# A delta-rule mixer whose level of 32 rows streams 128 columns per matmul instead of 64, with its banks of PSUM dealt out anew

## What is computed

```python
lmat = jnp.where(pos[:, None] > pos[None, :],
                 jnp.einsum('nbhid,nbhjd->nbhij', kb, kc) * decay, 0.0)
rhs = jnp.concatenate([vc * bc[..., None], kb * jnp.exp(gc)[..., None]], axis=-1)
sol = lax.linalg.triangular_solve(lmat, rhs, left_side=True, lower=True, unit_diagonal=True)
def step(s, inp):
    v_new = u_i - jnp.einsum('bhcd,bhde->bhce', w_i, s)
    s_next = s * gl_i[..., None, None] + jnp.einsum('bhcd,bhce->bhde', kd_i, v_new)
```

## Time and profile before

| | |
|---|---|
| median of three runs | 2609.36 us (2608.47 to 2612.84) |
| the profiled execution | 2613.24 us |
| its span, first to last instruction | 2611.4 us |
| TensorE matmul, busy | 2305.8 us (88%) |
| TensorE weight load, busy | 1528.2 us (59%) |
| VectorE, ScalarE, GpSimd, busy | 641.4, 475.2, 178.1 us |
| mean granted TensorE clock | 0.919 |
| `stage_delta`, first flip to the end of the chain | 1156.87 to about 1356 us |

### The profile page before, as it was taken

One profiled execution on the slowest core, in us unless ns is written; L12 is line 12 of the kernel. 1 busy time (PEld: TensorE's weight loads), 2 busy tenths in 40 slices (PEclk: granted clock), 3 DMA queues, 4 the chain that ended last, 5 costly groups with the idle time before them and its releaser, 6 DMA issues. The chain is left out here.

```text
span 2611.4 us, 26661 instructions
## 1 busy us (share of the span) xinstructions
PE 2305.8 (88%) x11220; PEld 1528.2 (59%) x11220; DVE 641.4 (25%) x1467; ACT 475.2 (18%) x879; POOL 178.1 (7%) x236
## 2 busy tenths in 40 slices
PE   6999696877999599889987899999979579999996
PEld 5855385565888475568876444454448444544453
DVE  2555112012220313652222211111110321111112
ACT  1222401112210224533331100000011110000000
POOL 1033001001110113300000000000000000000000
PEclk9999797998999799987787899999989879999998
DMA  6479542322442111010012899999944269999993
GB/s 191 159 257 334 198 170 72 125 69 66 160 163 69 65 65 65 33 65 1 1 44 118 342 427 427 428 427 427 427 185 161 97 259 427 427 427 428 427 427 157
DMA packets 120020, 575.55 MB, mean 220 GB/s; under 512 B 5153, under 2 KB 28282, under 8 KB 95322
## 3 DMA queue, kind: packets, MB, share of 16 engines
q1 hardware_dynamic: 118431, 570.59, 54.9%
q0 software_dynamic: 768, 2.02, 0.4%
q10 hardware_dynamic: 698, 1.18, 0.2%
HBM read 572.72 MB, written 1.05 MB: 220 GB/s over the span
## 5 line engine op out<-in xcount | busy, mean ns | idle before, releaser
L419 PE MATMUL linear_ps<-hT,ring 128*128 128x256 f32 x1344 | 300.2, 387 | 39.0 <-PEq L338 18.3
L419 PEld LDWEIGHTS linear_ps<-hT,ring 128*128 128x128 f32 x1344 | 260.6, 194 | 78.3 <-issue 41.7
L2423 PE MATMUL ex_u<-ring_extra,ex_xt 128*64 128x512 f32 x1024 | 224.9, 593 | 7.2 <-DMA ring_extra<-in_w 7.2
L2423 PE MATMUL ex_u<-ring,ex_xt 128*64 128x512 f32 x1024 | 225.0, 593 | 5.3 <-DMA ring<-in_w 3.9
L1657 PE MATMUL dl_front<-dn_src,ring 128*128 128x256 f32 (+1 forms) x512 | 177.5, 503 | 2.0 <-DVE dp_cv L1824 2.0
L2423 PEld LDWEIGHTS ex_u<-ring_extra,ex_xt 128*64 128x64 f32 x1024 | 76.3, 137 | 152.4 <-issue 152.2
L2423 PEld LDWEIGHTS ex_u<-ring,ex_xt 128*64 128x64 f32 x1024 | 78.0, 137 | 147.9 <-issue 147.9
L1106 PE MATMUL ffn_ps<-hT,ring 128*128 128x256 f32 x704 | 155.2, 384 | 5.9 <-PEq L338 5.9
L1106 PEld LDWEIGHTS ffn_ps<-hT,ring 128*128 128x128 f32 x704 | 135.8, 193 | 25.3 <-issue 6.3
L2512 DVE TENSOR_TENSOR ex_hid<-ex_sil,ex_u 128x512 f32<-128x512 f32 x32 | 34.6, 1081 | 435.9 <-PE ex_u L2423 435.9
L1657 PEld LDWEIGHTS dl_front<-dn_src,ring 128*128 128x128 f32 x512 | 99.3, 199 | 65.8 <-issue 58.9
(11 more groups left out here) (478 smaller groups left out, 2756.1 us busy)
## 6 DMA issues: line engine op xcount, KB each, us to landing
ring<-in_w SPq DMA_DIRECT2D x96, 2048.0 KB, 23.8
ring_extra<-in_w SPq DMA_DIRECT2D x96, 2048.0 KB, 25.1
ring<-in_ada_w SPq DMA_DIRECT2D x24, 2048.0 KB, 8.4
ring<-in_ffn_w_up SPq DMA_DIRECT2D x22, 1024.0 KB, 6.4
ring<-in_w_in SPq DMA_DIRECT2D x8, 2048.0 KB, 9.0
ring<-in_w_in_a SPq DMA_DIRECT2D x8, 2048.0 KB, 8.4
ring<-in_w_in_b SPq DMA_DIRECT2D x6, 2048.0 KB, 20.1
ring<-in_ffn_w_down SPq DMA_DIRECT2D x5, 2048.0 KB, 7.9
```

What stands on the lines that cost most here:

```text
L419: mm = pe.matmul(ps[:, q % banks, 0:n], w[:, k, j * P:(j + 1) * P], src[:, k, 0:n], start=k == 0, stop=k == kc - 1)
L2423: mm = pe.matmul(u[H * a:H * a + H, i, :], xt[:, b, k, H * a:H * a + H], w[a][:, 512 * k:512 * k + 512], start=k == 0, stop=k == KC - 1, s ...
```

## The change

Cross 0 and join 0 stream all 128 columns of `XN` and `XT` where they streamed two blocks of 32; the engines that read the products take the columns they want out of the wider tile, so they read as many elements as before. The results are placed in the full width of banks 5 and 3 (cross 0) and 4 and 5 (join 0). The near products of join 0 no longer fit beside them and move to the second half of bank 0, beside the output of the chain. Hence a new wait: from head 2 on, join 0 of head h waits until the output of head h-2 has been copied out. Cross 1 and join 1 keep their matmuls, in other banks. `part` goes. (The core of the diff; the reading sides of ScalarE and VectorE change in the same way.)

```diff
-        cross_ps = lambda k, d: ps[:, ((5, 3), (3, 4))[k][d], 0:T].rearrange("p (t n) -> p t n", t=4)
-        join_bank = lambda k, d: ((4, 5), (5, 3))[k][d]
-        join_ps = lambda k, d: ps[:, join_bank(k, d), 0:T].rearrange("p (t n) -> p t n", t=4)
-        near_ps = lambda d: ps[:, join_bank(0, d), T:T + P].rearrange("p (t n) -> p t n", t=4)
+        wide_cross_ps = lambda d: tiles_of(5 if d == 0 else 3)
+        cross_ps = lambda d: ps[:, 3 + d, 0:T].rearrange("p (t n) -> p t n", t=4)
+        wide_join_ps = lambda d: tiles_of(4 + d)
+        join_ps = lambda d: ps[:, 5 if d == 0 else 3, 0:T].rearrange("p (t n) -> p t n", t=4)
+        near_ps = lambda d: ps[:, 0, T + d * P:T + (d + 1) * P].rearrange("p (t n) -> p t n", t=4)
...
-                                mm = pe.matmul(cross_ps(k, d)[:, t, :], LT[g][:, m, :], part(d, XN[:, d, t, :]), start=True, stop=True)
+                                mm = pe.matmul(wide_cross_ps(d)[:, t, :], LT[g][:, m, :], XN[:, d, t, :], start=True, stop=True)
...
+                        elif h >= 2:
+                            pe.wait_ge(dl["o_taken"].sem, dl["o_taken"].at(h - 1))
...
-                                mm = pe.matmul(join_ps(k, d)[:, t, :], T1[:, k, d, t, :], part(1 - d, XT[g][:, m, :]), start=True, stop=True)
+                                mm = pe.matmul(wide_join_ps(d)[:, t, :], T1[:, k, d, t, :], XT[g][:, m, :], start=True, stop=True)
...
-                                ins = act.activation(T1[rows, k, d, :, cols], cross_ps(k, d)[rows, :, quad(i)], ACT.Copy)
+                                ins = act.activation(T1[rows, k, d, :, cols], wide_cross_ps(d)[rows, :, cols], ACT.Copy)
```

More of the change, by code:

```diff
@@ L1939, in stage_delta @@
         side_of = lambda i: slice(64 * i, 64 * i + 64)
-        def part(d, ap):
-            return ap.rearrange("p (a b n) -> p a b n", a=2, b=2)[:, :, d, :]
         @block.sync
@@ L1977, in _ @@
                             if k == 0:
-                                mm = pe.matmul(cross_ps(k, d)[:, t, :], LT[g][:, m, :], part(d, XN[:, d, t, :]), start=True, stop=True)
+                                mm = pe.matmul(wide_cross_ps(d)[:, t, :], LT[g][:, m, :], XN[:, d, t, :], start=True, stop=True)
                             else:
-                                mm = pe.matmul(cross_ps(k, d)[far, t, :], LT[g][near, m, far], XN[near, d, t, near], start=True, stop=True)
+                                mm = pe.matmul(cross_ps(d)[far, t, :], LT[g][near, m, far], XN[near, d, t, near], start=True, stop=True)
                         mm.then_inc(dl["z"].sem, dl["z"].tick())
@@ L1991, in _ @@
                                 pe.matmul(near_ps(d)[near, t, :], XT[g][near, m, near], T1[near, k, d, t, quad(3 * d)], start=True, stop=True)
-                                mm = pe.matmul(join_ps(k, d)[:, t, :], T1[:, k, d, t, :], part(1 - d, XT[g][:, m, :]), start=True, stop=True)
+                                mm = pe.matmul(wide_join_ps(d)[:, t, :], T1[:, k, d, t, :], XT[g][:, m, :], start=True, stop=True)
                             else:
-                                mm = pe.matmul(join_ps(k, d)[near, t, :], T1[far, k, d, t, near], XT[g][far, m, far], start=True, stop=True)
+                                mm = pe.matmul(join_ps(d)[near, t, :], T1[far, k, d, t, near], XT[g][far, m, far], start=True, stop=True)
                         mm.then_inc(dl["uv"].sem, dl["uv"].tick())
@@ L2056, in _ @@
                                 rows, cols = quad(2 * i + 1 - d), quad(2 * i + d)
[L2057 removed]
+                                ins = act.activation(T1[rows, k, d, :, cols], wide_cross_ps(d)[rows, :, cols], ACT.Copy)
                         else:
[L2059 removed]
+                            ins = act.activation(T1[side_of(1 - d), k, d, :, side_of(d)], cross_ps(d)[side_of(1 - d), :, :], ACT.Copy)
                         ins.then_inc(dl["t1"].sem, dl["t1"].tick())
@@ L2064, in _ @@
                         rows, cols = quad(2 * i + 1), quad(2 * i)
-                        act.activation(XT[g][rows, at(1, h):at(1, h) + 4, cols], join_ps(0, 1)[rows, :, quad(i)], ACT.Copy, scale=-1.0)
+                        act.activation(XT[g][rows, at(1, h):at(1, h) + 4, cols], wide_join_ps(1)[rows, :, cols], ACT.Copy, scale=-1.0)
                     act.activation(XN[quad(2), 1, :, quad(3)], near_ps(1)[quad(2), :, :], ACT.Copy,
@@ L2098, in _ @@
                         rows, cols = quad(2 * i), quad(2 * i + 1)
-                        dve.tensor_scalar(XT[g][rows, at(0, h):at(0, h) + 4, cols], join_ps(0, 0)[rows, :, quad(i)], -1.0, None, ALU.mult)
+                        dve.tensor_scalar(XT[g][rows, at(0, h):at(0, h) + 4, cols], wide_join_ps(0)[rows, :, cols], -1.0, None, ALU.mult)
                     dve.tensor_scalar(XN[quad(1), 0, :, quad(0)], near_ps(0)[quad(1), :, :],
@@ L2104, in _ @@
                         dve.wait_ge(dl["uv"].sem, dl["uv"].at(4 * h + 2 + d + 1))
-                        dve.tensor_scalar(XT[g][side_of(d), at(d, h):at(d, h) + 4, side_of(1 - d)], join_ps(1, d)[side_of(d), :, :],
+                        dve.tensor_scalar(XT[g][side_of(d), at(d, h):at(d, h) + 4, side_of(1 - d)], join_ps(d)[side_of(d), :, :],
                                           -1.0, None, ALU.mult).then_inc(dl["high"].sem, dl["high"].tick())
```

## The result

The changed kernel takes 2599.0 us in the median of 19 runs (2586.2 to 2604.4). The kernel before, run beside it, takes 2613.3 us in 19 runs (2608.4 to 2615.5). The ratio is 0.9944, with a 95% interval of 0.9932 to 0.9956: faster by 0.56%. The profiled execution took 2603.66 us against 2613.24 before, 9.6 us less. The runs of the changed kernel spread over 18 us where those of before spread over 7, and its profiled execution is one of its slower ones; the text comes back to that.

A forecast was written before the change was run, and what follows sets the result against it. TensorE bounds the stage, slowed by its clock, which falls in join 0. On the profiled execution 2613.2 - 5.0 - 8.4 + 1.2 = 2601.0; against the median 2609.4 - 12.2 = 2597 us, range 2581 to 2614.

The forecast's parts named there:

- a mixture of heads that keep the clock and heads that lose it: Join 0 of heads 2 to 7: half keep the clock, -8.4 us, half fall, +1.2 us; chance 0.40.
- Cross 0 costs nothing: Cross 0's 128 records go from 64 to 128 columns and keep flip's pace, 0.109 against 0.108 us.
- A pair costs 0.05 us more: Join 0's 64 near and far pairs: each 0.05 us longer at full clock, 0.10 at half clock.
- Banks, readers, wait: nothing: Readers between -0.05 and +0.05 us each; the wait on `o_taken` nothing, at most 12 waits of 0.05 us.
- A head that keeps its clock takes 21.0 us: Heads 2 to 7: 8.86 + 5.2 (join 0) + 6.98 (middle) = 21.0 us, 2.8 less than 23.8.
- A head that falls takes 0.4 us more than the mean of 23.8: Heads 2 to 7 that lose the clock about where they did: join 0 has 8 x 0.05 = 0.4 us more.
- Half of heads 2 to 7 keep it: Three heads keep the clock in join 0, 3 x -2.8 = -8.4 us; three fall, 3 x 0.4 = +1.2 us.
- Heads 0 and 1 gain 5.0 us: Cross 0 twice as dense before their fall: head 0 -1.4 us, head 1 1.0 regained and -2.6 us.
- all heads keep the clock: Rival: no head falls in join 0, heads 2 to 7 give -16.8 us, sum -26.1, 2583 us; chance 0.20.
- cross 1 and join 1 are thin: Doubt against all heads keeping the clock: both follow join 0, still on a quarter of the array, at a slack pace.
- The rival that the clock doesn't answer to columns: Rival: longer streams save no clock, pairs pay 0.05 or 0.10 us, +4.2 us, 2614 us; chance 0.11.
- change-overs: Join 0, doubt about keeping the clock: near products and change-overs still fill 0.28 of a pair's 0.65 us.

The follow-up runs named there:

- layout run: Changed kernel's banks, wait and readers, but cross 0 and join 0 both stream 64 columns again; 2609.6 us, ratio 0.9998 to the kernel before.
- the run with cross 0 alone: Changed kernel with join 0's far products back at 64 columns, cross 0 kept at 128; 2603.3 us, ratio 0.9975 to the kernel before.
- the grouped order: Changed kernel with, per direction of join 0, the four near products ahead of the four far ones; 2561.9 us, ratio 0.982 to the kernel before.
- the order grouped over both directions: Grouped kernel with both directions' near products ahead of both directions' far ones, 2 change-overs a head instead of 4; 2562.3 us, ratio 0.981.

## Why the prediction held, step by step

The forecast was 12.2 us less. Measured are 9.6 us less between the two profiled executions and 14.3 between the medians of 19 runs; 2599.0 us stands against the 2597 forecast. The mechanism is the one forecast, a mixture of heads that keep the clock and heads that lose it. That the number is so near is in part luck, for two reasons. A kept head was worth more than forecast and fewer heads were kept, and the two misses offset each other. And the distance between the medians depends on how the runs fall into groups: the kernel before has 5 of its 19 at 2608 to 2609 us and 14 at 2611 to 2615, the changed one 7 at 2603 to 2604, 7 at 2598 to 2601 and 5 at 2586 to 2589. Its first two groups lie about 10 us below the two of the kernel before, as the profiles do.

- *Cross 0 costs nothing.* Nearly so: 1.79 us instead of 1.73 for its 16 records in heads 2 to 7, and the read behind it is as much shorter. By my estimate from the Trainium skill (TensorE: Matmul & The Clock Gate, section "Back-to-back issue gap"), 27 ns a record, 16 records would have cost 0.43 us. The trace shows 0.06. That gap is the one the section gives for a matmul by itself; of a stream of weight loads and matmuls it says that both together set the spacing. The trace agrees with the latter: the columns doubled and the pace stayed, and it halves, to 0.056 us, where the same 64 columns meet quarter-size weights in cross 1.
- *A pair costs 0.05 us more.* 0.65 us at full clock, and in the layout run, with the new banks, a pair takes 0.60 (1255.17 to 1255.77), so none of it is the banks.
- *Banks, readers, wait: nothing.* Shown by the layout run, ratio 0.9998 (0.9989 to 1.0007).
- *A head that keeps its clock takes 21.0 us.* It takes 19.97. The terms that were too long are those of the middle, for which I had no full-clock row at full length. Cross 1 and join 1 take 0.90 and 0.89 us instead of 1.17 each, for my row of join 1 was in part at half clock. State 1 and read 2 take 1.5 with their waits where I had 1.84, and new 2 takes 1.20 where I had 1.35. Join 0 is 5.08 for 5.2, and state 2 alone is longer, 1.54 for 1.45.
- *A head that falls takes 0.4 us more than the mean of 23.8.* The four took 23.86, 23.85, 24.90 and 24.91 us, 24.4 in the mean: 0.6 more.
- *Half of heads 2 to 7 keep it.* Two of six in both profiles of the changed kernel. With 3.9 us each instead of 2.8, and the others' 0.6, heads 2 to 7 come to -5.4 where I had -7.2.
- *Heads 0 and 1 gain 5.0 us.* 4.4, and the run with cross 0 alone shows what it is made of: -6.5 by cross 0's columns, and +2.2 when join 0's come on top. The reason that I gave, cross 0 twice as dense, is the right one.

Of the rivals, that all heads keep the clock (2583) was close to what some executions may do: 5 of the 19 runs of the changed kernel took 2586 to 2589 us. Their granted clocks over the whole span, 0.930 to 0.933 against 0.922 to 0.926 in the others, say that they kept it longer somewhere; 12 us are three heads at 3.9. No profile fell on one of them, so it stays open which heads they keep, or whether it is heads at all. Against this rival I had held that cross 1 and join 1 are thin. That was wrong: in no profile does one of heads 2 to 7 lose its clock there; all the falls lie in join 0 or within 0.2 us of its end. The rival that the clock doesn't answer to columns is excluded by the layout run against the changed kernel. The Trainium skill (TensorE: Matmul & The Clock Gate, section "Why this matters for your kernels") asks only for no gaps between bursts of matmuls. The trace disagrees: in join 0 of head 2 TensorE was busy for 4.78 of 4.78 us up to the fall, so avoiding gaps that a profile shows is not enough.

What the prediction saw and undervalued is the change-overs. I counted 0.28 of the 0.65 us of a pair as near products and change-overs, and used that only as a doubt. Taking most of them out is worth 32 to 37 us beyond the change, more than twice what the change itself brought.

## What to carry to other kernels

Where TensorE is busy and still loses its clock, look for the stretch before the fall and ask what fills its time. Here full-size float32 records started as slowly with 64 columns as with 128, and each change between sizes of the array cost 0.15 us that the profile still counts as busy. Group the small products, or give them the full array, before adding columns; then add columns where a timeline shows that they don't change the pace of the records, for there they are free. A gain that hangs on keeping a clock comes in whole steps, here 3.9 to 4.9 us a head, so it must be judged from many runs, and a profile of one run shows which steps that run got.

## What the runs showed of the hardware

- Float32 records of 64 and of 128 columns with full weights start at the same pace at full clock, 1.73 / 16 = 0.108 and 1.79 / 16 = 0.112 us; quarter-array records of 64 columns start every 0.90 / 16 = 0.056 us.
- After a change of the array's size the columns show: 64 more cost a pair 0.05 us. The starts of the records have all of it between the two far ones (0.21 us for 0.16) and none behind the second (0.2 us in both).
- A pair of a quarter-array and a full product takes 0.65 us, and 0.45 if both are full; 12 fewer change-overs make join 0 1.84 us shorter.
- Twice the columns in join 0 alone slowed heads 0 and 1 by 2.3 us, at a clock of 0.62 and 0.55. Of that, 1.9 us are join 0 itself, mostly or all at half clock: 8.18 us for 7.16 in head 0 and 8.45 for 7.59 in head 1.
- Best of all kernels run: the grouped order at 2561.9 us, the one with near products on the full array at 2563.1, and the order grouped over both directions at 2562.3. Their intervals overlap. All beat the kernel before by 1.8 to 1.9% and, by the ratios, the changed one by 1.2 to 1.4%.
